# The end of a hybrid S5 and retention block: last matmul steps bank by bank, half of the norm moved, three rows added by transfers

## What is computed

```python
def rms_norm(x, gain):
    y = x * lax.rsqrt(jnp.mean(x * x, axis=-1, keepdims=True) + EPS)
    return y * gain

h    = rms_norm(x, norm_pre)
proj = h @ w_in                      # u_s, z_s, q, k, v, z_r, gl_s, gl_r
y_s  = s5_mixer(u_s, ...) * silu(z_s)
y_r  = retention(q, k, v) * silu(z_r)
m    = sigmoid(gl_s) * (y_s @ w_proj_s5) + sigmoid(gl_r) * (y_r @ w_proj_ret)
x    = x + rms_norm(m @ w_out, norm_post)
```

## Time and profile before

| | us |
|---|---|
| median of 3 runs | 2223.32 |
| the profiled execution | 2223.09 |
| its span, first to last instruction | 2221.3 |
| TensorE busy in the span | 2177.6 |
| VectorE busy | 1787.4 |
| ScalarE busy | 1169.6 |
| last matmuls begin | 2202.09 |
| last store issued, end of span | 2217.6, 2221.3 |

### The profile page before, as it was taken

How to read it: one execution, slowest core, us unless ns; L and a number is a source line. 1 busy time by engine, 2 the same in 40 slices (tenths; PEclk the granted TensorE clock), 3 DMA queues, 4 the chain that set the end, 5 groups by cost and what they waited for, 6 DMA issues and landing times.

```text
span 2221.3 us, 28657 instructions
## 1 busy us (share of the span) xinstructions
PE 2177.6 (98%) x10288; PEld 1805.3 (81%) x10288; DVE 1787.4 (80%) x2915; ACT 1169.6 (53%) x1966; POOL 127.2 (6%) x201
## 2 busy tenths in 40 slices
PE   8999999999999999999999999999999999999996
PEld 6687888888888888888888888988888888788885
DVE  5997997977898887876877866767788889986778
ACT  6644445455665454465555554845545545455554
POOL 6044001000000000000000000200000000000000
PEclk9999999999999999999999999999999999999998
DMA  9577568686586465588774989576845756744557
GB/s 374 224 234 248 155 226 282 230 278 213 181 282 189 154 221 163 189 300 302 251 227 133 318 256 299 154 244 209 289 146 195 246 176 190 256 150 135 185 160 281
DMA packets 268815, 496.61 MB, mean 224 GB/s; under 512 B 51920, under 2 KB 60112, under 8 KB 265984
## 3 DMA queue, kind: packets, MB, share of 16 engines
q1 hardware_dynamic: 221408, 409.55, 55.6%
q10 hardware_dynamic: 37568, 50.44, 6.6%
q0 software_dynamic: 9696, 34.78, 5.0%
HBM read 378.29 MB, written 116.39 MB: 223 GB/s over the span
## 4 chain that ended last, share of the span: by engine, by line
PE 76%; DVE 12%; DMA 4%; issue 3%; POOL 2%; SPq 2%; ACT 2%; DVEq 0%; ACTq 0%; POOLq 0%
PE psum L2010 55%; PE psum L2007 18%; DVE a_lo L1452 2%; DVE b_lo L1454 2%; DMA araw<-aops 2%; POOL work L778 1%; DVE work L1712 1%; DVE work L1408 1%; DMA work<-in_xT 1%; DVE work L1765 1%; PE psum L2028 1%; DVE keep L1462 1%; PE psum L2111 0%; PE psum L2046 0%; ACT a_hi L1008 0%
## 5 line engine op out<-in xcount | busy, mean ns | idle before, releaser
L1008 ACT ACTIVATE a_hi<-araw 128x512 fp32r<-128x512 f32 x644 | 405.9, 630 | 854.6 <-PE psum L2010 622.8
L1452 DVE TENSOR_TENSOR a_lo<-araw,a_hi 128x512 fp32r<-128x512 f32 x644 | 443.6, 689 | 321.4 <-ACT a_hi L1008 318.6
L2010 PE MATMUL psum<-a_hi,b_hi 128*128 128x512 f32 x2352 | 632.1, 390 | 8.0 <-ACT b_hi L1017 6.5
L2010 PE MATMUL psum<-a_lo,b_hi 128*128 128x512 f32 x2352 | 632.0, 390 | 5.0 <-DVE a_lo L1452 4.4
L2010 PE MATMUL psum<-a_hi,b_lo 128*128 128x512 f32 x2352 | 629.0, 389 | 0.0
L2010 PEld LDWEIGHTS psum<-a_lo,b_hi 128*128 128x128 f32 x2352 | 440.5, 188 | 103.2 <-DVE a_lo L1452 11.7
L2010 PEld LDWEIGHTS psum<-a_hi,b_hi 128*128 128x128 f32 x2352 | 441.3, 188 | 102.1 <-ACT b_hi L1017 6.9
L2010 PEld LDWEIGHTS psum<-a_hi,b_lo 128*128 128x128 f32 x2352 | 441.7, 188 | 92.3
L1454 DVE TENSOR_TENSOR b_lo<-bx,b_hi 128x512 fp32r<-128x512 f32 x432 | 296.6, 687 | 0.0
L1017 ACT ACTIVATE b_hi<-bx 128x512 fp32r<-128x512 f32 x432 | 266.4, 617 | 1.3 <-DMA bx<-in_wstream 1.2
L2007 PE MATMUL psum<-b_hi,a_lo 128*128 128x512 f32 x672 | 180.4, 390 | 4.7 <-DVE a_lo L1452 4.7
(11 more groups left out here) (185 smaller groups left out, 1575.6 us busy)
## 6 DMA issues: line engine op xcount, KB each, us to landing
araw<-aops SPq DMA_DIRECT2D x632, 256.0 KB, 3.1
bz<-in_wstream SPq DMA_DIRECT2D x224, 256.0 KB, 4.5
aops<-work SPq DMA_DIRECT2D x28, 1024.0 KB, 6.7
spill<-keep ACTq DMA_DIRECT2D x28, 1024.0 KB, 5.9
bx<-in_wstream SPq DMA_DIRECT2D x108, 256.0 KB, 4.8
by<-in_wstream SPq DMA_DIRECT2D x108, 256.0 KB, 5.4
work<-spill SPq DMA_DIRECT2D x20, 1024.0 KB, 7.6
aops<-work POOLq DMA_DIRECT2D x15, 1024.0 KB, 5.9
```

The source lines that it names most:

```text
L1008: A.activation(a_hi[:, r, :], left(s), ACT.Copy, scale=gain).then_inc(head, 1)
L1452: V.tensor_tensor(a_lo[:, r, :], left(s), a_hi[:, r, :].bitcast(F32), ALU.subtract).then_inc(split, 1)
L2010: done = T.matmul(bank, b[:, r, cols], a[:, r, :], start=first and part == 0, stop=last and part == 2, skip_group_check=on)
```

## The change

There are four parts.

1. The last two steps of the kernel (at 54 and 55) are multiplied bank by bank: for bank 0 the three pairings of step 54 and the three of step 55, then the same for banks 1 to 3 (`multiply_last`). Each bank signals `bank_done`. ScalarE's squares and VectorE's gains of product 6 wait for one bank each. The sums, roots and inverses of rows 4 and 5 are apart from those of 6 and 7 (`ROWS_OF`).
2. For rows 0 to 3 the work is on other steps: product 5 is evacuated ahead of the rests of at 50 and no longer behind them, squares are at 50 and 51, the gain at 50, the sum at 51, the inverse and row 0 at 52, row 1 in halves at 53 and 55. A root of a constant at 36 of the group makes ScalarE load its table there.
3. Rows 2, 3 and 5 are no longer finished by VectorE. ScalarE multiplies them by the inverse root (`scale_row`, a copy with a scale, by halves of 128x1024), and GpSimd's queue adds each half onto `out` in HBM with an adding transfer. So that x is there, SyncE's queue copies x rows 2, 3 and 5 from HBM to HBM at 12, 18 and 24; the loads of these rows into SBUF are gone.
4. All stores are by halves: ten for rows 0, 1, 4, 6 and 7.

```diff
+ROWS_OF = (slice(0, 4), slice(4, 6), slice(6, 8))
...
+                if g == GO1 and at in (12, 18, 24):
+                    n = {12: 2, 18: 3, 24: 5}[at]
+                    sp.dma_start(out[n], x[n]).then_inc(late_loaded, 16)
...
+            for n, piece in enumerate((0, 0, 1, 1, 4, 4, 6, 6, 7, 7)):
                 sp.wait_ge(rows_ready, n + 1)
+                sp.dma_start(out[piece][:, half_row(n % 2)], o_row[:, piece, half_row(n % 2)]).then_inc(out_stored, 16)
...
+            pool.wait_ge(late_loaded, 5 * 16)
+            for n, row in enumerate((2, 2, 3, 3, 5, 5)):
+                pool.wait_ge(row_scaled, n + 1)
+                pool.dma_start(out[row][:, half_row(n % 2)], o_row[:, row, half_row(n % 2)], accum_op=ALU.add
+                               ).then_inc(row_added, 16)
+            pool.wait_ge(row_added, 6 * 16)
...
+            def root_rows(i):
+                act.wait_ge(rows_normed, 2 * i + 1)
+                A.activation(rstd_out[:, ROWS_OF[i]], rstd_out[:, ROWS_OF[i]], ACT.Sqrt, scale=1.0 / D_MODEL,
+                             bias=eps_sb[:, 0:1]).then_inc(out_std, 1)
+
+            def scale_row(n, half):
+                act.wait_ge(rows_normed, {2: 2, 3: 2, 5: 4}[n])
+                act.wait_ge(gained, {2: 7, 3: 7, 5: 9}[n])
+                A.activation(o_row[:, n, half_row(half)], o_row[:, n, half_row(half)], ACT.Copy, scale=rstd_out[:, n:n + 1]
+                             ).then_inc(row_scaled, 1)
...
+                if s == BASE[GO1] + 36:
+                    A.activation(x_rstd[:, 0, 0:1], eps_sb[:, 0:1], ACT.Sqrt)
+                if s == BASE[GO1] + 53:
+                    root_rows(0)
+                    scale_row(2, 0)
+                    scale_row(2, 1)
+                if s == STEPS - 1:
+                    scale_row(3, 0)
+                    scale_row(3, 1)
+                if s == STEPS:
+                    squares(GO1, 6, 0, 1)
+                    squares(GO1, 6, 1, 1)
+                    root_rows(1)
+                    squares(GO1, 6, 2, 1)
+                    scale_row(5, 0)
+                    squares(GO1, 6, 3, 1)
+                    root_rows(2)
+                    scale_row(5, 1)
...
+            def gain_bank(n):
+                col = COLS * (2 + COL_OF[KEEP[6]])
+                dve.wait_ge(bank_done, n + 1)
+                dve.wait_ge(out_squared, 28 + n + 1)
+                V.tensor_tensor(o_row[:, 4 + n, col:col + COLS], main_banks(GO1)[:, n, :], gain_row[:, col:col + COLS],
+                                ALU.mult).then_inc(gained, 1)
...
+                if ended(s - 3) == (GO1, 5):
+                    evacuate(GO1, 5)
                 if s < STEPS:
                     rests(s)
...
+                if g == GO1 and at == 50:
+                    take_rows(GO1, 5)
+                if g == GO1 and at == 51:
+                    sum_rows(0)
+                if g == GO1 and at == 52:
+                    invert_rows(0)
+                    finish_row(0, 0)
+                    finish_row(0, 1)
+                if g == GO1 and at in (53, 55):
+                    finish_row(1, (at - 53) // 2)
...
                 if s == STEPS:
-                    finish_row(2)
-                    finish_row(3)
-                    take_rows(GO1, 6)
+                    gain_bank(0)
+                    gain_bank(1)
+                    sum_rows(1)
                     invert_rows(1)
-                    for n in range(4, 8):
-                        finish_row(n)
+                    finish_row(4, 0)
+                    gain_bank(2)
+                    sum_rows(2)
+                    gain_bank(3)
+                    invert_rows(2)
+                    finish_row(4, 1)
+                    for n in (6, 7):
+                        finish_row(n, 0)
+                        finish_row(n, 1)
...
+            def multiply_last():
+
+                for n in range(4):
+                    cols = slice(P * n, P * n + P)
+                    for s in (STEPS - 2, STEPS - 1):
+                        r = s % RING
+                        for part in range(3):
+                            if part == 0:
+                                pe.wait_ge(head, 2 * s + 2)
+                            else:
+                                pe.wait_ge(split, 2 * s + part)
+                            a = a_lo if part == 1 else a_hi
+                            b = b_lo if part == 2 else b_hi
+                            done = T.matmul(main_banks(GO1)[:, n, :], a[:, r, cols], b[:, r, :], start=False,
+                                            stop=s == STEPS - 1 and part == 2, skip_group_check=True)
+                    done.then_inc(bank_done, 1)
```

More of the change, by code:

```diff
@@ L348, in build_program, with half_row @@
         rows_ready, out_stored = sem("rows_ready"), sem("out_stored")
+        bank_done, row_scaled, row_added = sem("bank_done"), sem("row_scaled"), sem("row_added")
         block = ctx.enter_context(nc.Block())
+        def half_row(n):
+            return slice(D_MODEL // 2 * n, D_MODEL // 2 * (n + 1))
         def kept(b):
@@ L743, in _ @@
-                if g == GO1 and at in (53, 55):
-                    n = (at - 45) // 2
-                    sp.wait_ge(split, 2 * (step_of(g, 5, TILES[g] - 1) + 1))
-                    sp.wait_ge(summed, sums_before(g, 6, TILES[g] - 1) + 1)
-                    sp.dma_start(x_rest[n], x[n]).then_inc(late_loaded, 16)
-            for n in range(4):
-                sp.wait_ge(rows_ready, n + 1)
-                sp.dma_start(out[n], o_row[:, n, :]).then_inc(out_stored, 16)
-            for n in range(4, 8):
-                for half in range(2):
-                    sp.wait_ge(rows_ready, 2 * n - 3 + half)
-                    cols = slice(D_MODEL // 2 * half, D_MODEL // 2 * (half + 1))
-                    sp.dma_start(out[n][:, cols], o_row[:, n, cols]).then_inc(out_stored, 16)
@@ L1120, in squares @@
                 if (g, p) == (GO1, 6):
-                    act.wait_ge(step_done, STEPS)
+                    act.wait_ge(bank_done, first + 1)
                 elif p == 6:
@@ L1246, in _ @@
                 over = ended(s - 5)
-                if ended(s - 4) == (GO1, 5) or ended(s - 5) == (GO1, 5):
-                    squares(GO1, 5, 2 * (s - BASE[GO1] - 51), 2)
-                elif ended(s - 1) == (GO1, 6):
-                    squares(GO1, 6)
-                elif over and over[1] >= 3 and over != (GO1, 6):
+                if ended(s - 3) == (GO1, 5) or ended(s - 4) == (GO1, 5):
+                    squares(GO1, 5, 2 * (s - BASE[GO1] - 50), 2)
+                elif over and over[1] >= 3 and over not in ((GO1, 5), (GO1, 6)):
                     if over[0] in (GO0, GO1):
@@ L1754, in finish_row @@
[L1754 to L1766 removed]
+                V.reciprocal(rstd_out[:, ROWS_OF[i]], rstd_out[:, ROWS_OF[i]]).then_inc(rows_normed, 1)
@@ new lines, in finish_row @@
+            def finish_row(n, half):
+                dve.wait_ge(rows_normed, {0: 2, 1: 2, 4: 4, 6: 6, 7: 6}[n])
+                dve.wait_ge(gained, {0: 7, 1: 7, 4: 8, 6: 10, 7: 11}[n])
+                dve.wait_ge(rows_loaded[int(n in (1, 6))], {0: 48, 1: 48, 4: 64, 6: 64, 7: 80}[n])
+                cols = half_row(half)
+                V.scalar_tensor_tensor(o_row[:, n, cols], o_row[:, n, cols], rstd_out[:, n:n + 1], x_sum_rows[n][:, cols],
+                                       ALU.mult, ALU.add).then_inc(rows_ready, 1)
@@ L1797, in _ @@
                 over = ended(s - 3)
-                if over and over[1] in dve_takes(over[0]) and over != (GU, 5):
+                if over and over[1] in dve_takes(over[0]) and over not in ((GU, 5), (GO1, 5)):
                     evacuate(*over)
```

76 lines of the change are left out of this document (21 added, 55 removed).

## The result

The changed kernel takes 2225.89 us in the median of 22 runs (2222.73 to 2230.16), the kernel before 2222.1 beside it. The ratio is 1.0014, with a 95% interval from 1.0009 to 1.002: slower by 2.0 to 4.4 us. The ratio leaves out one of the 22 executions of the kernel before, a far slower one of 2603.66 us.

The account below looks back on a forecast made before the run. TensorE was taken as busy until its last matmul, with VectorE and the transfers both full behind it. Last landing 2217.3, plus 0.4 for the span (2217.7), plus 1.8 gave 2219.5 us; range 2215.3 to 2225.5.

Parts of the forecast that it names:

- Part 3, the transfers: Stores at the end: five plain halves from 2207.5 at 1.29 us and one adding half at 1.9, last landing 2217.3.
- rival A: At the end, transfers have room and VectorE's chain sets the time: 2217.2 to 2217.8, or 2216.6 or less; chance 0.24.
- Part 2: At 50 to 55: moved norm work costs TensorE nothing and takes about 7 us from VectorE behind the last rests.
- Part 1: Last two steps, bank by bank: 0.3 us of TensorE stall for b_lo of at 55, possible range nothing to 1 us.
- ScalarE's half row: Scaling one half row of 128x1024 on ScalarE takes 1.12 us, between 0.9 and 1.44; square 3 waits behind (5,0).
- VectorE's last half: End of VectorE's chain: its last half row ends at 2212.3, 5.25 us before 2217.55.
- Rival C: At 12, 18 and 24, copies hold up operand loads; TensorE loses 4.0 us three times, 2231.5 us; chance 0.09.
- Rival D: At 52 to 55, the shorter cover breaks and TensorE stops 1 to 3 us: 2220.5 to 2222.5; chance 0.09.
- Rival B: Between the last stores, row 5's adding halves cost four stores, 5.2 us each, landing over 7 us: 2225.4; chance 0.08.

Follow-up runs that it names:

- a3: Changed kernel with only rows 2 and 3 added by transfer, row 5 written plain without its x: 2223.65 us, ratio 1.0003 against the kernel before.
- m1: Kernel before, followed by batches of GpSimd transfers alone: in batches of four, 1.34 us for a plain half and 2.88 for an adding one.
- a1: Changed kernel with GpSimd's six transfers plain, x of rows 2, 3 and 5 left out: 2219.3 us, ratio 0.9985 against the kernel before.
- b1: Kernel before with the three HBM to HBM copies of x added at 12, 18 and 24: 2223.68 us, ratio 0.9999 against the kernel before.
- a2: Changed kernel with only row 5 added by transfer, rows 2 and 3 written without x: 2222.1 us, ratio 0.9995 against the kernel before.
- b3: Changed kernel without its third part, all eight rows finished by VectorE and stored by halves: 2222.87 us, ratio 0.9999 against the kernel before.
- c1: Changed kernel with only row 2 added by transfer, rows 3 and 5 finished by VectorE: 2221.38 us, ratio 0.9993; timed again, 2221.04 us, ratio 0.999.
- b4: Kernel before with only the third part of the change (copies, ScalarE scaling, six adding halves): 2229.76 us, ratio 1.0028 against the kernel before.

## Why the prediction was wrong, step by step

**The failed step is "Part 3, the transfers", the bill of the adding halves.** It puts one adding half of six into the sum and prices it at 1.9 us; measured it is 2.76 after, and all six stand in the sum. Its last sentence, "Adding transfers of rows 2 and 3 are long done by then", is false: in a3 these four alone cost 4.5 us of the tail. And it starts the bill too late ("the plain stores (4,1) from 2207.5 on", and "the transfers are idle before 2207.5" in rival A). The earlier trace rows show only the very end, and I took the time ahead of it for idle. The trace of the kernel before shows that the four whole rows already fill the transfers there (columns as above):

```profile
2200.00:2204.00 4.00, 3.16 (x14) 2.27 (x13) 4.00 (x3) 0.77 (x3) 0.00 (x0) 1.00 0.79 326
2204.00:2208.00 4.00, 0.00 (x0) 0.00 (x0) 3.96 (x8) 2.28 (x7) 0.00 (x0) 0.96 1.01 420
```

**Number and price have to be right together.** After, the first store goes out 5.0 us ahead of the first matmul of at 54, and 0.8 us go into the start and the end. With all six adding halves at the 1.9 us that I chose the bill is 10 x 1.29 + 6 x 1.9 = 24.3 us, and the tail 24.3 - 5.0 + 0.8 = 20.1: the forecast again, by coincidence, because two errors of the forecast (five halves left out, the bill begun late) cancel at that price. With the right price for (5,1) alone the forecast grows by 0.9 us. With both, 10 x 1.35 + 6 x 2.76 = 30.1 us, the tail is 25.9, which is what was measured. The price makes 5.2 us of the difference, because it is paid six times, and the plain stores 0.6.

The price was 1.5 stores taken, 2.05 measured after and 2.15 in m1. The Trainium skill's rule that the prediction weighed (Collectives: The Full Stack, the bandwidth ceiling: two source reads, half the rate) has the size right. The page states it for reductions between cores, and no run here shows the two reads. By the prediction's sum it gave only 2220.1, because it too was applied to one transfer; with 2.6 us for each of the six the tail is 24.3. Another page of the Trainium skill, DMA: Bandwidth & Descriptors, section "Issuing engines are not separate DMA queues", says that transfers of all engines run on the same 16 and interleave. The trace agrees: SyncE's ten plain stores land after 9.9 us in the median after, where GpSimd's six transfers add, and after 4.5 in a1, where they are plain.

**Part 2 (nothing lost in at 50 to 55)** was right: at 48 to at 54 takes 16.32 us in both. **Part 1**: a weight load waited 0.16 us for b_lo of at 55, and the matmuls lost less than that (0.3 taken). The last matmul begins 5.26 us behind the first of at 54 (2195.06 to 2200.32), where before it was 5.21. **ScalarE's half row** was 1.14 us in the end and 2.18 for a pair (1.12 taken), and square 3 does wait for (5,0), to 2201.41. **VectorE's last half** ends 13.86 us behind the first matmul of at 54, forecast 14.74: the last inverse is earlier than I had it.

**Rival C** (copies stop TensorE) is refuted by b1. **Rival D** (the shorter cover breaks) by the 16.32. **Rival A** (VectorE's chain sets the end) comes near in a1, where the addition is gone: a tail of 18.9 against its 18.4 (2216.0 less 2197.56). **Rival B** (adding transfers stand in the way) is the nearest to what happened, with other sizes: it took four stores for one adding half where it is two, and one and a half such halves in the way where it is six. That its price of 2225.4 lies so near the measured 2225.89 is luck, since both factors are off and in opposite directions. Its sign, a last landing over 7 us, came true: 11.6 for the store issued last.

**What stays open.** By the tails after is 2.1 us longer than before, by the medians 3.8 (2.0 to 4.4 by the ratio, which holds both). For all kernels with parts 1 and 2 (after, a1, a2, a3, b3 and c1 twice) the median, against that of before beside it, comes out 0.6 to 1.7 us less good than the tail. For b1 it is 0.2, and for b4, which lacks parts 1 and 2, it is 1.1 us better. The last group up to at 54 is not the place: it takes the same 146.88 us before and after, the root's table load at 36 included. What is left is the stretch ahead of the last group, in which no step was changed and whose end varies by 5.4 us between these profiles, or tails of executions that weren't profiled. No run here tells these apart.

## What to carry to other kernels

Before moving work from an engine to transfers, write down the bill of the transfers from the first one of the stretch to the last, all queues together: each transfer's bytes at the plain rate, an adding one twice. If the queue runs empty in between, start a new bill there; a2, where I didn't, came out 2.4 us over the sum. If that sum is longer than the chain that it relieves, move fewer. Here one row of three was faster than before (c1), and in a3 four adding halves already made a tail of 23.4 us against 20.9. Other splits were not run. An early transfer is not free because it is early: it is free only if the queue is empty again when the late ones come.
